# Expert and mark tables of a routed FFN's load loop interleaved, and six words of a step pair read by one load

## The chip, the cores and the metric

One core of one Trainium2 chip runs the whole program. The metric is the device time of one execution in microseconds (us). The runs of the kernel before took 1639.86, 1643.22 and 1646.82 us, median 1643.22.

## The reference

One layer on 512 latent tokens and 256 context tokens of width 1024: a bidirectional gated linear recurrence (HGRN2), then an expert FFN, then a final RMS norm. The part that matters here is the expert FFN: each token goes to 4 of 32 experts.

```python
logits = (h @ router_w + router_b)
top_v, top_i = lax.top_k(logits, 4)
top_w = softmax(top_v)
# for the tokens of an expert e:
z_glu, z_lin = split(h[tok] @ w1[e] + b1[e])        # w1[e]: 1024 x 2048
act = z_glu * sigmoid(1.702 * z_glu) * (z_lin + 1)   # both halves clamped at 7
y = act @ w2[e] + b2[e]                              # w2[e]: 1024 x 1024
```

The results are added per token with their weights. All is float32, so an expert's weights are 12 MB (8 MB of w1, 4 MB of w2) and those of all 32 are 384 MB.

## The kernel before

**Stages.** The recurrence and the router take the first 520 us or so. Then comes the expert loop, up to about 1592 us, and last the sum of the four results per token and the norm.

**Blocks, steps and two sides.** Tokens are grouped by expert in blocks of 32 slots (`G`). The 32 experts are put in two lists of 16 in an order worked out on the chip, by their number of blocks. One list goes through the *even* steps (`par` 0), whose weights lie in `arena`; the other through the *odd* steps (`par` 1), whose weights lie in `big_b`. A pair of steps is one turn of the loops `Fori(0, n_pairs)` that TensorE, VectorE, ScalarE, GpSimd (POOL) and SyncE (SP) each run; here it has 42 turns, 84 steps. An expert with several blocks stays in its side's buffer for several turns.

**The slots.** A side holds one expert in 12 slots of 1 MB: eight for w1 (`w1_slot`), four for w2 (`w2_slot`). In a step TensorE (L1805 to L1829) uses the last two w1 slots of the step (`z_chunk`, L1788), adds the bias (L1812), runs the first six w1 slots of the next step, which is the other side's, and then the four w2 slots of its own (L1826). After each slot it raises `w1_used` or `w2_used`, and before each it waits for that slot's load semaphore (`ld_w1`, `ld_w2`).

**SP's loop** (L475 to L505) issues the weight loads of both sides, one queue, in program order. At the head of each step it reads four words with `entry(1)` and `entry(2)` (L478 to L484): the expert of the next step and whether it is new there (the *mark*), and the same of the step after that, which is this side's next. They come from two tables of 192 words in one partition, `tab_l` (experts, clamped to 31) and `tab_new` (marks). A `value_load` with `min_val` and `max_val` is a load into a register followed by a check. After the head: `over_w1(0, 6)` waits for each of this side's first six w1 slots to be used and loads the side's next expert into it (L487 to L490, issued at L429), if the mark says that it is new; otherwise it only raises the load semaphore (L491 to L494). Then the same for the four w2 slots of the other side (L497 to L504, issued at L435), then `over_w1(6, 8)`.

**The tables** are written by VectorE before the loop (L1340 to L1348), from `bef`, the expert of each step: `tab_e`, `tab_l`, `tab_nf` and from it `tab_new`; `tab_ok` releases SP. SP gets there after its early weight loads (L444 to L471).

**POOL** gathers the token rows of the step after next (L621, into `xg`; VectorE transposes them at L1234 for TensorE) and scatters the results (L627).

Of the kernel before, what the change touches and what calls it, by code (L numbers as in the profile page):

```python
# [7 lines left out]
I32 = mybir.dt.int32  # L8
U32 = mybir.dt.uint32
F32R = mybir.dt.float32r  # L10
ALU = mybir.AluOpType
# [11 lines left out]
E, TOPK = 32, 4  # L23
# [4 lines left out]
NBT = 2 * NPAIR_MAX + 4  # L28
# [9 lines left out]
NW = D // QT  # L38
# [24 lines left out]
def build(nc, x, c, ctx_in, c_ctx, mod_c, mod_w, mod_b, norm1_g, norm2_g, hg_w_in, hg_lb_logits, hg_norm_g,  # L63
# [7 lines left out]
    with ExitStack() as stack:  # L71
        place = {}

        def sb(name, shape, dt=F32):
            place[name] = -(-nc.sbuf_base // 32) * 32
            return stack.enter_context(nc.sbuf_tensor(name, shape, dt))
# [20 lines left out]
        at = [0]  # L97
# [49 lines left out]
        res = sb("res", [P, 2, TOK], BF16)  # L147
# [26 lines left out]
        def rtake(n):  # L174
            at2[0] += n
            return ring_t[:, at2[0] - n:at2[0]]
# [21 lines left out]
        def half(n):  # L198
# [15 lines left out]
        bef = sb("bef", [P, NBT])  # L214
        ed_t = bef[0:E, 0:E]
        tab_e = sb("tab_e", [1, NBT], I32)
        tab_l, tab_new = (nc.alloc_sbuf_tensor_at(n, [1, NBT], I32, offset=place["res"] + 4 * NW + 4 * i * NBT)
                          for i, n in enumerate(("tab_l", "tab_new")))
        tab_nf = rtake(NBT)[0:1]
        tab_nn = sb("tab_nn", [1, 2])  # L220
        tab_n = sb("tab_n", [1, 2], I32)
# [117 lines left out]
        def _(sp):  # L339

            row = 0
            for v in (c[0], c_ctx, mod_b, norm1_g, hg_lb_logits[0, 0], hg_lb_logits[0, 1],
                      hg_lb_logits[1, 0], hg_lb_logits[1, 1], hg_norm_g):
                n = v.shape[0] // P
# [83 lines left out]
            def load_w1(par, e, pos):  # L428
                sp.dma_start(w1_slot(par, pos), moe_w1[bass.ds(e * D + pos * P, P), :]  # L429
                             ).then_inc(ld_w1[par][pos], 16)  # L430

            def load_w2(par, e, k):
                to = w2a[:, 2 * k:2 * k + 2, :] if par == 0 else \
                    big_b[:, B2_AT[k], :].rearrange("p (a n) -> p a n", a=2)
                sp.dma_start(to, moe_w2[bass.ds(e * FF + 2 * k * P, 2 * P), :].rearrange("(a p) n -> p a n", p=P)  # L435
                             ).then_inc(ld_w2[par][k], 16)
# [36 lines left out]
            n_pairs = sp.value_load(tab_n[0:1, 0:1], min_val=1, max_val=NPAIR_MAX)  # L473

            with sp.Fori(0, n_pairs) as i:  # L475
                for par in range(2):

                    def entry(n):  # L478
                        at = bass.ds(i * 2 + (par + n), 1)
                        return (sp.value_load(tab_l[0:1, at], min_val=0, max_val=E - 1),  # L480
                                sp.value_load(tab_new[0:1, at], min_val=0, max_val=1))

                    e_next, new_next = entry(1)
                    e_over, new_over = entry(2)  # L484

                    def over_w1(first, last):
                        with sp.If(new_over):  # L487
                            for pos in range(first, last):
                                sp.wait_ge(S["w1_used"], i * (2 * W1C) + (par * W1C + pos + 1))
                                load_w1(par, e_over, pos)  # L490
                        with sp.Else():  # L491
                            for pos in range(first, last):
                                sp.wait_ge(S["w1_used"], i * (2 * W1C) + (par * W1C + pos + 1))
                                sp.sem_inc(ld_w1[par][pos], 16)  # L494

                    over_w1(0, AHEAD)
                    with sp.If(new_next):  # L497
                        for k in range(W2C):
                            sp.wait_ge(S["w2_used"], i * (2 * W2C) + (par * W2C + k + 1))
                            load_w2(1 - par, e_next, k)  # L500
                    with sp.Else():
                        for k in range(W2C):
                            sp.wait_ge(S["w2_used"], i * (2 * W2C) + (par * W2C + k + 1))
                            sp.sem_inc(ld_w2[1 - par][k], 16)  # L504
                    over_w1(AHEAD, W1C)  # L505
# [373 lines left out]
        def _(dve):  # L879
            V = nc.vector  # L880
            me = Steps(dve, S["dve_s"])
# [409 lines left out]
            for i in range(LT):  # L1291
# [47 lines left out]
            dve.wait_ge(S["tab_ps"], 6)  # L1339
            me.link(V.tensor_scalar(bef[:, :], ps[7][:, 0:NBT], float(E), None, ALU.add))  # L1340
            me.mark(V.tensor_copy(tab_e[:, :], bef[0:1, :]))
            me.mark(V.tensor_scalar(tab_l[:, :], bef[0:1, :], float(E - 1), None, ALU.min))
            me.mark(V.tensor_tensor(tab_nf[:, 2:NBT], bef[0:1, 2:NBT], bef[0:1, 0:NBT - 2], ALU.not_equal))
            me.wait()
            me.link(V.scalar_tensor_tensor(tab_nf[:, 2:NBT], bef[0:1, 2:NBT], float(E) - 0.5, tab_nf[:, 2:NBT],
                                           ALU.is_lt, ALU.mult))
            me.link(V.tensor_copy(tab_new[:, :], tab_nf))
            dve.sem_inc(S["tab_ok"], 1)  # L1348
            dve.wait_ge(S["xi_ps"], 2)
            index(1, False)  # L1350
# [57 lines left out]
            me = Steps(dve, S["fin_s"])  # L1408
# [479 lines left out]
```

## Time and profile before

| | |
|---|---|
| median of the runs | 1643.22 us |
| profiled execution | 1641.11 us, span 1638.9 us |
| granted TensorE clock, mean | 0.951 of full |
| PE busy | 1485.2 us (91%) |
| DVE, ACT, POOL busy | 734.8 (45%), 251.8 (15%), 211.9 (13%) |
| bytes moved by DMA | 497.14 MB, mean 303 GB/s |
| weight loads, L429 and L435 | 384 issues of 1024 KB |
| chain that ended last | PE 62%, DMA 22%, SPq 9%, DVE 4%, issue 3% |

Engines: PE is TensorE, DVE VectorE, ACT ScalarE, POOL GpSimd; SPq is SyncE's instruction queue, which has no busy time of its own, since it only issues, waits and computes registers. The busy share is an average over stages with different limits; the chain of waits is followed back from the last instruction. Times in a timeline are microseconds from the start of the span. A transfer in the chain reaches from its issue to its landing, with what it waits for other transfers of its queue counted in. A matmul in float32 is two instructions in the trace, so a slot's four matmuls are eight rows.

### The profile page before, as it was taken

The numbers are of one execution on the slowest core, as the hardware profiler recorded it, in microseconds if no ns is written. First come the engines' busy times: TensorE is split into PE (matmuls) and PEld (weight loads), VectorE is DVE, ScalarE is ACT, GpSimd is POOL, SyncE is SP. The second block draws the span as 40 slices with busy tenths as digits, with TensorE's granted clock in tenths as the row PEclk, the third lists the DMA queues.
The fourth block names the chain that finished last, engine by engine and source line by source line (L and its number), as shares of the span: only waits on it lengthen the run. The fifth ranks groups of instructions, "written<-read, shape, count | busy, mean of one in ns | idle before, by whom it ended". The sixth has DMA issues, their size and how long they took to land.

```text
span 1638.9 us, 40839 instructions
## 1 busy us (share of the span) xinstructions
PE 1485.2 (91%) x14640; PEld 739.0 (45%) x14640; DVE 734.8 (45%) x2468; ACT 251.8 (15%) x434; POOL 211.9 (13%) x263
## 2 busy tenths in 40 slices
PE   5999999999894988999899799999788979898897
PEld 3658888888552332333244234333233323343233
DVE  4403877776747442434244244434233424343344
ACT  4403554554322000000000000000000000000001
POOL 1000000000250111212121111212111211111120
PEclk9999999999996998999799799999899989999898
DMA  8685111112767898948989989999899989999788
GB/s 358 194 269 146 52 52 51 51 51 55 277 266 265 338 419 320 417 199 337 414 325 400 414 336 400 417 414 412 320 418 416 417 324 410 417 413 417 298 323 310
DMA packets 130870, 497.14 MB, mean 303 GB/s; under 512 B 15372, under 2 KB 48492, under 8 KB 94908
## 3 DMA queue, kind: packets, MB, share of 16 engines
q1 hardware_dynamic: 122588, 479.99, 74.3%
q0 software_dynamic: 8256, 16.81, 2.8%
q8 instruction: 16, 0.26, 0.1%
q14 instruction: 10, 0.08, 0.0%
HBM read 484.92 MB, written 17.58 MB: 307 GB/s over the span
## 4 chain that ended last, share of the span: by engine, by line
PE 62%; DMA 22%; SPq 9%; DVE 4%; issue 3%; ACT 1%; POOL 0%; DVEq 0%; POOLq 0%; ACTq 0%
PE ps L1788 22%; PE ps L1826 12%; DMA arena<-in_moe_w 10%; DMA big_b<-in_moe_w 10%; PE ps L1485 6%; PE ps L1487 5%; PE ps L1486 5%; SPq L435 3%; SPq L429 3%; PE ps L1664 2%; PE ps L1596 1%; PE ps L1508 1%; DMA ring_t<-in_mod_c 1%; PE ps L1610 1%; PE ps L1605 1%
## 5 line engine op out<-in xcount | busy, mean ns | idle before, releaser
L1788 PE MATMUL ps<-arena,rows 128*32 128x512 f32 x2736 | 330.2, 617 | 41.8 <-DMA arena<-in_moe_w 33.4
L1788 PE MATMUL ps<-big_b,rows 128*32 128x512 f32 x2688 | 318.7, 609 | 29.6 <-DMA big_b<-in_moe_w 29.2
L1788 PEld LDWEIGHTS ps<-arena,rows 128*32 128x32 f32 x2736 | 86.4, 112 | 239.3 <-issue 151.2
L862 ACT ACTIVATE rows<-ps 128x256 f32<-128x256 f32 x84 | 32.3, 385 | 1050.1 <-issue 566.3
L1788 PEld LDWEIGHTS ps<-big_b,rows 128*32 128x32 f32 x2688 | 85.0, 111 | 220.2 <-issue 149.0
L1826 PE MATMUL ps<-big_b,rows 128*32 128x256 f32 x2688 | 166.4, 398 | 15.3 <-DMA big_b<-in_moe_w 15.3
L1826 PE MATMUL ps<-arena,rows 128*32 128x256 f32 x2688 | 167.0, 400 | 13.8 <-DMA arena<-in_moe_w 13.8
L1403 DVE SCALAR_TENSOR_TENSOR y_sb<-ps,w_s,g_q 128x256 f32<-128x256 f32 x42 | 20.3, 484 | 293.2 <-PE ps L1826 293.2
L1403 DVE SCALAR_TENSOR_TENSOR rows<-ps,w_s,g_q 128x256 f32<-128x256 f32 x42 | 20.3, 484 | 279.0 <-PE ps L1826 279.0
L1826 PEld LDWEIGHTS ps<-big_b,rows 128*32 128x32 f32 x2688 | 84.2, 114 | 77.6 <-DMA big_b<-in_moe_w 21.7
L1826 PEld LDWEIGHTS ps<-arena,rows 128*32 128x32 f32 x2688 | 84.8, 114 | 75.7 <-DMA arena<-in_moe_w 20.3
L621 POOL DMA_INDIRECT rows<-frows,tok_n x86 | 88.6, 1030 | 105.4 <-issue 59.2
L1485 PE MATMUL ps<-aT_hi,wh_hi 128*128 128x512 f32 x256 | 101.7, 397 | 0.0
L1487 PE MATMUL ps<-aT_hi,wh_lo 128*128 128x512 f32 x256 | 99.8, 390 | 0.0
L1486 PE MATMUL ps<-aT_lo,wh_hi 128*128 128x512 f32 x256 | 99.8, 390 | 0.0
L627 POOL DMA_INDIRECT yrows<-y_sb,row_s x43 | 44.2, 1029 | 421.0 <-issue 421.0
L627 POOL DMA_INDIRECT yrows<-rows,row_s x43 | 45.0, 1047 | 413.1 <-issue 412.2
L1273 DVE TENSOR_SCALAR pt<-slot_io,dm_all 128x128 bf16<-128x128 f32 x344 | 75.3, 282 | 33.2 <-issue 33.2
L563 POOL TENSOR_SCALAR xv_t<-xv_t 96x1024 f32<-96x1024 f32 x1 | 2.8, 2791 | 433.5 <-DMA xv_t<-in_moe_b 433.5
L1487 PEld LDWEIGHTS ps<-aT_hi,wh_lo 128*128 128x128 f32 x256 | 48.0, 188 | 10.3
L1485 PEld LDWEIGHTS ps<-aT_hi,wh_hi 128*128 128x128 f32 x256 | 48.1, 188 | 10.0
L1486 PEld LDWEIGHTS ps<-aT_lo,wh_hi 128*128 128x128 f32 x256 | 48.1, 188 | 9.1
(361 smaller groups left out, 1769.6 us busy)
## 6 DMA issues: line engine op xcount, KB each, us to landing
big_b<-in_moe_w SPq DMA_DIRECT2D x192, 1024.0 KB, 15.4
arena<-in_moe_w SPq DMA_DIRECT2D x192, 1024.0 KB, 16.7
ring_t<-in_hg_w_in SPq DMA_DIRECT2D x32, 512.0 KB, 3.9
ogT<-in_mod_w SPq DMA_DIRECT2D x16, 1024.0 KB, 5.1
arena<-yrows SPq DMA_DIRECT2D x8, 1024.0 KB, 12.0
x_sb<-in_x SPq DMA_DIRECT2D x2, 2048.0 KB, 7.9
arena<-in_hg_w_in SPq DMA_DIRECT2D x4, 1024.0 KB, 21.0
arena<-in_mod_c SPq DMA_DIRECT2D x4, 1024.0 KB, 22.3
```

Source lines behind the costliest of these rows:

```text
L429: sp.dma_start(w1_slot(par, pos), moe_w1[bass.ds(e * D + pos * P, P), :]).then_inc(ld_w1[par][pos], 16)
L435: sp.dma_start(to, moe_w2[bass.ds(e * FF + 2 * k * P, 2 * P), :].rearrange("(a p) n -> p a n", p=P)).then_inc(ld_w2[par][k], 16)
L621: pool.indirect_dma_start(out=xg[par], out_offset=None, in_=fquarters, in_offset=bass.IndirectOffsetOnAxis(ap=tok_n[par][:, :], axis=0), b ...
L627: pool.indirect_dma_start(out=yquarters, out_offset=bass.IndirectOffsetOnAxis(ap=row_s[par][:, :], axis=0), in_=y_sb[par], in_offset=None, ...
L1273: V.tensor_scalar(to[:, i, :], slot_io[:, :], dm_all[:, i, e], None, ALU.is_equal)
L1403: V.scalar_tensor_tensor(y_sb[par], ps[4 + par][:, 0:NW], w_s[par][:, :], g2_q[:, :], ALU.mult, ALU.mult).then_inc(S["y_ok"], 1)
L1485: mm(bank, th, mh, start=start, stop=False)
L1486: mm(bank, th, ml, start=False, stop=False)
L1487: return mm(bank, tl, mh, start=False, stop=stop)
L1664: last = mm(ps[YO_BANK[j]][:, :], ogT[:, k, i * P:(i + 1) * P], wo[n][:, k, :], start=(k == 0), stop=(k == DK - 1))
L1788: last = mm(bank[q * G:(q + 1) * G, :], XT[par][:, pos * G:(pos + 1) * G], w[:, :, q * NW:(q + 1) * NW], start=(pos == 0), stop=False)
L1826: last = mm(y[q * G:(q + 1) * G, 0:NW], aT2[:, (2 * m + a) * G:(2 * m + a + 1) * G], w2_slot(par, m, a)[:, q * NW:(q + 1) * NW], start=(m ...
```

## The change

- `tab_l` and `tab_new` become one table `tab_words`, two words per step (expert, mark), with two words of room in front, in the same place.
- VectorE writes the two halves with a step of two words; values are the same.
- SP no longer reads four words at the head of each step; it reads six words at the head of each pair, with one load instruction into six registers: expert and mark of steps 2i+1, 2i+2 and 2i+3. The even step uses words 0 to 3, the odd step 2 to 5.
- The check of each value against its bounds is left out.

```diff
--- before.py
+++ after.py
@@ -214,8 +214,8 @@
         bef = sb("bef", [P, NBT])
         ed_t = bef[0:E, 0:E]
         tab_e = sb("tab_e", [1, NBT], I32)
-        tab_l, tab_new = (nc.alloc_sbuf_tensor_at(n, [1, NBT], I32, offset=place["res"] + 4 * NW + 4 * i * NBT)
-                          for i, n in enumerate(("tab_l", "tab_new")))
+        tab_words = nc.alloc_sbuf_tensor_at("tab_words", [1, 2 * NBT + 2], I32, offset=place["res"] + 4 * NW)
+        tab_ld = tab_words[:, 2:2 * NBT + 2].rearrange("p (b w) -> p b w", w=2)
         tab_nf = rtake(NBT)[0:1]
         tab_nn = sb("tab_nn", [1, 2])
         tab_n = sb("tab_n", [1, 2], I32)
@@ -473,15 +473,13 @@
             n_pairs = sp.value_load(tab_n[0:1, 0:1], min_val=1, max_val=NPAIR_MAX)
 
             with sp.Fori(0, n_pairs) as i:
+                _, words = nc.values_load_multi_w_load_instructions(
+                    tab_words[0:1, bass.ds(i * 4 + 4, 6)], engines=[mybir.EngineType.SP], min_val=0, max_val=E - 1,
+                    skip_runtime_bounds_check_because="experts are clamped to E - 1 and marks are 0 or 1 where written")
                 for par in range(2):
 
-                    def entry(n):
-                        at = bass.ds(i * 2 + (par + n), 1)
-                        return (sp.value_load(tab_l[0:1, at], min_val=0, max_val=E - 1),
-                                sp.value_load(tab_new[0:1, at], min_val=0, max_val=1))
-
-                    e_next, new_next = entry(1)
-                    e_over, new_over = entry(2)
+                    e_next, new_next = words[2 * par:2 * par + 2]
+                    e_over, new_over = words[2 * par + 2:2 * par + 4]
 
                     def over_w1(first, last):
                         with sp.If(new_over):
@@ -1339,12 +1337,12 @@
             dve.wait_ge(S["tab_ps"], 6)
             me.link(V.tensor_scalar(bef[:, :], ps[7][:, 0:NBT], float(E), None, ALU.add))
             me.mark(V.tensor_copy(tab_e[:, :], bef[0:1, :]))
-            me.mark(V.tensor_scalar(tab_l[:, :], bef[0:1, :], float(E - 1), None, ALU.min))
+            me.mark(V.tensor_scalar(tab_ld[:, :, 0], bef[0:1, :], float(E - 1), None, ALU.min))
             me.mark(V.tensor_tensor(tab_nf[:, 2:NBT], bef[0:1, 2:NBT], bef[0:1, 0:NBT - 2], ALU.not_equal))
             me.wait()
             me.link(V.scalar_tensor_tensor(tab_nf[:, 2:NBT], bef[0:1, 2:NBT], float(E) - 0.5, tab_nf[:, 2:NBT],
                                            ALU.is_lt, ALU.mult))
-            me.link(V.tensor_copy(tab_new[:, :], tab_nf))
+            me.link(V.tensor_copy(tab_ld[:, :, 1], tab_nf))
             dve.sem_inc(S["tab_ok"], 1)
             dve.wait_ge(S["xi_ps"], 2)
             index(1, False)
```

## Rows read from the trace of the kernel before

**Rows 1.** TensorE's waits, 540 to 1592: waiter, releaser: us in total, times, longest.
```profile
PE ps L1788 <- DMA arena<-in_moe_w: 33.4, 28, 2.3
...
PE ps L1788 <- DMA big_b<-in_moe_w: 29.2, 26, 2.3
...
PE ps L1826 <- DMA big_b<-in_moe_w: 15.3, 16, 1.5
...
PE ps L1826 <- DMA arena<-in_moe_w: 13.8, 15, 1.5
```

**Rows 2.** Stretches: length, busy us by engine, clock, DMA share, GB/s.
```profile
547.00:645.00 98.00, 82.98 (x932) 28.91 (x924) 32.45 (x149) 2.70 (x7) 14.37 (x14) 0.91 0.98 400
...
953.00:1080.00 127.00, 122.23 (x1496) 48.06 (x1492) 51.60 (x236) 4.22 (x11) 22.59 (x22) 0.97 1.00 407
...
1185.00:1344.00 159.00, 136.46 (x1564) 48.79 (x1556) 52.22 (x239) 4.23 (x11) 22.58 (x22) 0.92 1.00 409
...
1352.00:1445.00 93.00, 88.82 (x1080) 33.99 (x1076) 36.88 (x167) 3.08 (x8) 16.44 (x16) 0.96 1.01 412
...
1553.00:1592.00 39.00, 39.00 (x504) 16.01 (x500) 15.38 (x71) 1.15 (x3) 6.17 (x7) 1.00 0.82 333
...
716.00:745.00 29.00, 29.00 (x368) 11.46 (x364) 13.71 (x62) 1.15 (x3) 6.16 (x6) 1.00 0.06 20
```

**Rows 3.** Timeline 843 to 849: start, us, engine, line, operation, count.
```profile
845.50 4.05 PE L1788 MATMUL ps<-big_b,rows 128*32 128x512 f32 x36
...
848.39 0.35 SPq L429 DMA_DIRECT2D big_b<-in_moe_w  x1
```

**Rows 4.** Timeline 1180 to 1187, TensorE and SP.
```profile
1181.20 5.33 PE L1788 MATMUL ps<-arena,rows 128*32 128x512 f32 x48
...
1184.77 2.23 SPq L429 DMA_DIRECT2D arena<-in_moe_w  x4
```

**Rows 5.** Chain of waits, 900 to 1010: start, us, queue, line.
```profile
919.75 0.07 SPq L475
...
922.35 0.05 SPq L487
...
923.45 0.05 SPq L499
...
923.71 0.39 SPq L435
```

**Rows 6.** Lines 480 and 481 on SP: count: ns min/median/max, first and last.
```profile
L480 SPq TENSOR_LOAD <-tab_l x168: 262/270/589, 538.8 to 1582.8; - x168
...
L481 SPq FUSED_REGOPS  x168: 147/147/157, 539.8 to 1584.0; - x168
```

**Rows 7.** Timeline 505 to 548, VectorE, the second table write.
```profile
520.02 0.25 DVE L1347 CAST tab_new<-ring_t 1x192 int32<-1x192 f32 x1
```

**Rows 8.** Timeline of SP's transfers, 530 to 1600; x is how many were issued.
```profile
536.33 0.37 SPq L435 DMA_DIRECT2D arena<-in_moe_w  x1
...
536.74 0.99 SPq L435 DMA_DIRECT2D big_b<-in_moe_w  x2
...
546.63 5.63 SPq L429 DMA_DIRECT2D big_b<-in_moe_w  x8
...
1017.76 8.38 SPq L429 DMA_DIRECT2D big_b<-in_moe_w  x8
...
1445.53 8.00 SPq L429 DMA_DIRECT2D arena<-in_moe_w  x8
```

**Rows 9.** Line 429, loads of w1: time from issue to landing.
```profile
DMA to landing us min/median/max: 4.7/15.1/26.0
```

**Rows 10.** Timeline 814 to 824, a gather and the transpose that uses it.
```profile
814.29 1.04 POOL L621 DMA_INDIRECT rows<-frows,tok_n  x1 [0.70 <-issue]
...
822.48 0.43 DVE L1234 STREAM_TRANSPOSE rows<-rows 128x256 f32<-128x256 f32 x1
```

**Rows 11.** Line 621, the gathers: time from issue to landing.
```profile
DMA to landing us min/median/max: 2.6/6.0/6.7
```

## The prediction

> **What bounds the kernel now.** I read four views, in this order. The waits of TensorE in the expert loop name one releaser only, the weights: 33.4 + 29.2 + 15.3 + 13.8 = 91.7 us in 85 waits [rows 1]. So the loop is either at TensorE's own pace or waiting for weights. Cutting the loop by hand into stretches shows that these alternate [rows 2]. In a stretch with weights the 16 DMA engines are full (share 0.98 to 1.01, 400 to 412 GB/s) and TensorE is idle for part of it: 15.0 us of 547 to 645, 4.8 of 953 to 1080, 22.5 of 1185 to 1344, 4.2 of 1352 to 1445. Between them lie dry stretches, 716 to 745 the longest, with 20 GB/s and TensorE never idle: the experts in work need no new weights, and both buffers are full. The reader is to see that nothing can be gained inside a full stretch (the bytes set it) and nothing inside a dry one (TensorE sets it), but that the end of a dry stretch counts: when the first load of the next expert is issued earlier, the whole train of loads behind it lands earlier, and the wait that ends the train shrinks by as much. I call such a point a restart.
>
> What holds a restart back is seen in the timeline. At 845.50 TensorE starts the 48 matmuls of six chunks that use up six slots; the first 36 take 4.05 us, so a chunk of eight takes 0.90 us and the first slot is free at 846.40. The first load into it is issued by SP at 848.39 [rows 3]. At the next restart of the other buffer it is 1181.20 + 0.89 (48 in 5.33 us, six chunks) = 1182.09 against 1184.77 [rows 4]. SP is late by 2.0 and 2.7 us. What it does in that time is the head of the step, read off the chain of waits where it shows a whole one: from the top of the loop at 919.75 to the first branch at 922.35, 2.60 us [rows 5].
>
> **What the change removes.** A head has four table loads. Each is a load of 0.27 us (median of 168, two such groups), a register operation of 0.147 us [rows 6], and an assertion, an address and gaps for the rest of 0.62 us; four make 2.5, and with the loop's own 0.1 the 2.60 above. Over 84 steps that is 84 x 2.5 = 210 us of SP's time; it is not the gain, since SP mostly waits or is blocked.
>
> **What it adds.** One load of six words per pair of steps. No row shows a load of more than one word. Lower bound: as one word, 0.27. Upper bound: six single ones, 1.6, the words being fetched one after the other. The longest single one was 0.59 [rows 6]. I take 0.4, near the single row, since what an instruction of this kind spends is mostly its trip; without the checks one register wait of up to 0.15 may stay. So the head of an even step (arena, behind the loop's branch) goes from 2.6 to some 0.5, and that of an odd step (big_b) to nothing.
> A rule of the Trainium skill speaks against this: "Runtime: NRT & Kernel Launch", section Instruction fetch mechanics, puts a register load at about 200 ns per register even in bulk, though from HBM; by it the six words would be an estimated 1.2 us and the sum below 2.4 us smaller. No row here shows which holds. Another, in "DMA: Bandwidth & Descriptors", Latency and other measured facts, puts the floor of such a load at some 600 ns; the trace does not agree, 0.262.
>
> The two table writes on VectorE get a step of two words. The second takes 0.25 us [rows 7]; if the stride costs up to as much again, that is 0.5 us for both, and less than nothing is excluded, as no element falls away. They are done at 520.3, while SP is busy with earlier weights until 537.73 [rows 8] and reads the tables only then: I take nothing. If SP came sooner, they would cost 0.5 us once.
>
> **What a restart gains.** The release of a slot to the issue costs SP a computed address, a move and the issue: 923.45 to 923.71 where the chain shows it, 0.3 us with the semaphore [rows 5].
> - Odd step: possible at 846.40 + 0.3 = 846.7, was 848.39: **1.7 us**.
> - Even step: the slot allows 1182.4. SP's head began at 1184.77 - 0.4 - 2.6 = 1181.8; with 0.5 and 0.4 it issues at 1182.7: **2.1 us**.
>
> Which first loads are restarts follows from counting. An expert is 12 loads of 1.049 MB, 2.57 us each at 408 GB/s; the quickest load landed 4.7 us after its issue [rows 9]. A train of n loads begun at T is thus through at T + 4.7 + 2.57(n - 1), and the next load lands 2.57 later or 4.7 after its own issue, whichever is later. Only in the second case does the issue matter. SP's timeline has 16 first issues that qualify or come close; going through them:
> - 546.63 (odd). Three loads from 536.33 on end near 546.2; the next could land at 548.7, but 546.63 + 4.7 = 551.3 [rows 8]. Two heads lie between SP's last early issue and this one, 2.1 + 2.5 = 4.6 us earlier: limited by the queue to 2.6, I take **2.4**.
> - 650.80 and 744.41 (odd, dry before): **1.7** each.
> - 848.39 (odd), then 881.76 (even): 848.39 + 33.0 = 881.4, the queue just runs out, so the even restart decides: **2.1**.
> - 952.46, 985.67, 1017.76: each 33 us on, the queue just empty each time. At 1017.76 (odd, [rows 8]) pace alone gives 1021.2, the issue 1022.5; the lead passes through and the odd one caps it: **1.7**.
> - 1080.83, then 1112.77 (odd): the same, **1.7**.
> - 1184.77 (even, dry): **2.1**. Its train runs on to 1344; at 1243.40 and 1277.27 the queue is not empty, nothing more.
> - 1351.23 (even, dry): **2.1**.
> - 1445.53 (even, [rows 8]): 36 loads from 1351.23 end at 1445.9, the next by pace 1448.5, by issue 1450.2; part of the three trains was blocked by a full queue, so I take **1.0**.
> - 1552.41 (even, dry): TensorE is busy in 39.0 of the last 39.0 us [rows 2], nobody waits for this train: **0**.
>
> Sum: 2.4 + 1.7 + 1.7 + 2.1 + 1.7 + 1.7 + 2.1 + 2.1 + 1.0 = **16.5 us**. Each is smaller than TensorE's idle time in its train (4.2 us at least), so none is lost to the pace of TensorE. The gains add, because after each train TensorE sets the time of the next restart from the landing before it. The profiled execution took 1641.1 us (span 1638.9 and 2.2 around it): 1624.6. The median of the runs, 1643.2, is 2.1 above it; less 16.5 it is **1626.7, I say 1627**.
>
> **Rivals.**
> 1. The words are fetched one by one, 1.6 us. The even head is then 0.1 + 1.6 + 0.15 instead of 2.6, the even restart gains 0.9 and not 2.1. The three even ones that decide lose 3 x 1.2 = 3.6, the odd ones nothing: gain 13, 1630. For it: no row of a multi-word load; against: 0.27 for one word cannot tell trip from words. Chance 0.17.
> 2. The transfers don't move. The first load may be late for a reason that a shorter head leaves: a stall of SP at the branch into the rarely run issuing arm, or a train paced by slots and not by the queue. For it: the chain of waits never names the head at a restart. Against: that chain follows a late load to its own issue and counts the queue before it as transfer, so it can't name it. Gain 0 to 8 us, 1635 to 1643. Chance 0.15.
> 3. Slower: the gathers. POOL fetches the next rows right at a restart (814.29, used at 822.48, 8.2 us [rows 10]); in dry stretches such a gather has the engines for itself, and now 1.7 to 2.1 us more of each restart's weights stand before it. From a landing of over 8.2 us on, TensorE waits in every step in a full stretch. Landings are 2.6 to 6.7 us at present, those of full stretches included [rows 11], so it would take 1.5 us more than the worst. If each of some 45 steps in full stretches lost 0.7 us, that is 31 less 16: 1658. Chance 0.03.
> 4. The removed checks are put back by the build, so that only the loads merge. Then six register operations with their assertions stay, 6 x 0.2 = 1.2 us on the even head, and the odd restarts gain all the same: like the first rival, 1629. It shares its chance.
>
> **How the numbers follow.** Forecast 0.65, within 1622 to 1632. The first rival (and fourth) adds 1629 to 1633, the second 1635 to 1643, the third above. About half of the second must be left out: 1619 to 1638. Under 0.5% (8.2 us, about what a measurement tells from no change) falls most of rival 2 and a thin end of the others: faster 0.80, same 0.16, slower 0.04.
>
> **What would show it.** The last stretch (1553 to 1592) has TensorE never idle as before, and the dry stretches keep their length less 1.7 to 2.1 us each. First issues come 1.2 us after the start of the six chunks at odd restarts and 1.5 at even ones, in place of 2.9 and 3.6. TensorE's 91.7 us of waits fall to about 75; matmul times, bytes and the full rate stay. A table load group of 42, once per pair, shows its length: 0.4 or 1.6 decides rival 1. I am wrong if the first issues move and the waits don't, or if waits for the gathers' transpose appear.

## The result, and the profile after

The changed kernel takes 1628.0 us (median, 1624.45 to 1632.99), the kernel before 1642.5 (1639.86 to 1646.82) beside it: a ratio of 0.9926, 95% interval 0.9903 to 0.9950. That is 12.2 us less by the ratio, 8.2 to 15.9 by its interval; the medians alone differ by 14.5. 1627 was predicted, from a sum of 16.5. So the gain came out at three quarters of the sum, and that the median lies within 1 us of 1627 is in part luck.

The profiled execution took 1632.99 us with a span of 1630.8. The first rows of its page, busy time and the 40 slices, differ from those of the kernel before in a place here and there only:

```profile
PE 1487.4 (91%) x14640; PEld 742.2 (46%) x14640; DVE 737.1 (45%) x2468; ACT 251.7 (15%) x434; POOL 211.8 (13%) x263
...
PE   5999999999995997999799799999889979998897
...
PEclk9999999999997997999899799999798989998898
...
DMA  8685111112767798957989989999899989999778
...
GB/s 359 201 266 146 52 52 51 51 51 56 267 258 287 317 419 334 417 215 325 414 338 404 414 340 402 417 415 418 332 417 416 417 329 417 417 413 417 314 309 307
```

TensorE's waits in the expert loop, as in [rows 1]:

```profile
PE ps L1786 <- DMA arena<-in_moe_w: 33.4, 27, 2.3
...
PE ps L1786 <- DMA big_b<-in_moe_w: 24.9, 22, 2.2
...
PE ps L1824 <- DMA arena<-in_moe_w: 11.7, 14, 1.5
...
PE ps L1824 <- DMA big_b<-in_moe_w: 11.5, 14, 1.5
```

They add up to 81.5 us, 10.2 less than 91.7; a fall to about 75 was predicted. The reader is to see that busy times say nothing here (PE 1487.4 against 1485.2, at a mean granted clock of 0.945 against 0.951); the time went out of the waits for weights.

The first issues in SP's timeline, as in [rows 8]:

```profile
544.18 6.05 SPq L429 DMA_DIRECT2D big_b<-in_moe_w  x8
...
947.23 10.10 SPq L429 DMA_DIRECT2D big_b<-in_moe_w  x8
...
1012.42 10.11 SPq L429 DMA_DIRECT2D big_b<-in_moe_w  x8
...
1072.38 9.74 SPq L429 DMA_DIRECT2D arena<-in_moe_w  x8
...
1435.54 9.76 SPq L429 DMA_DIRECT2D arena<-in_moe_w  x8
```

And an odd and an even restart, each with the bias matmul, which starts 0.22 us before the six chunks, as in [rows 3, 4]. First the odd one, then the even one:

```profile
842.61 0.40 PE L1810 MATMUL ps<-bias,sel 96*32 96x512 bf16 x4
...
844.10 1.19 SPq L429 DMA_DIRECT2D big_b<-in_moe_w  x2
```

```profile
1175.97 0.40 PE L1810 MATMUL ps<-bias,sel 96*32 96x512 bf16 x4
...
1177.82 0.96 SPq L429 DMA_DIRECT2D arena<-in_moe_w  x2
```

The first load now follows the start of the bias matmul by 1.49 us at an odd step and by 1.85 at an even one. In the kernel before it was 3.11 and 3.79, read in the same way (bias at 845.28 and 1180.98). So odd restarts come 1.62 us earlier relative to TensorE and even ones 1.94; 1.7 and 2.1 had been worked out. The load of six words:

```profile
L476 SPq TENSOR_LOAD <-tab_words x42: 714/720/1088, 540.5 to 1563.0; - x42
```

It took 0.72 us (the median; the three numbers are least, median and most in ns), between the 0.4 taken and the 1.6 of the first rival.

### The profile page after: what moved, and what is told of

Read it like the earlier page. It is cut to its first block, busy times and chain, and to the rows that moved or that the text cites. A ratio compares the mean times of both kernels' runs of the same rounds, so it can differ in the third digit from the quotient of the medians.

```text
span 1630.8 us, 39663 instructions
## 1 busy us (share of the span) xinstructions
PE 1487.4 (91%) x14640; PEld 742.2 (46%) x14640; DVE 737.1 (45%) x2468; ACT 251.7 (15%) x434; POOL 211.8 (13%) x263
## 4 chain that ended last, share of the span: by engine, by line
PE 65%; DMA 20%; SPq 8%; DVE 4%; issue 2%; ACT 1%; POOL 0%; DVEq 0%; POOLq 0%; ACTq 0%
PE ps L1786 25%; PE ps L1824 12%; DMA big_b<-in_moe_w 9%; DMA arena<-in_moe_w 8%; PE ps L1483 6%; PE ps L1484 5%; PE ps L1485 5%; SPq L435 5%; SPq L429 2%; PE ps L1662 2%; PE ps L1506 1%; PE ps L1594 1%; DMA ring_t<-in_mod_c 1%; PE ps L1603 1%; PE ps L1608 1%
## 5 line engine op out<-in xcount | busy, mean ns | idle before, releaser
L1824 PEld LDWEIGHTS ps<-big_b,rows 128*32 128x32 f32 x2688 | 84.8, 114 | 74.0 <-DMA big_b<-in_moe_w 17.2
L1485 PEld LDWEIGHTS ps<-aT_hi,wh_lo 128*128 128x128 f32 x256 | 48.1, 188 | 10.2
```

Of the source, the lines that this page charges most:

```text
L1485: return mm(bank, tl, mh, start=False, stop=stop)
L1824: last = mm(y[q * G:(q + 1) * G, 0:NW], aT2[:, (2 * m + a) * G:(2 * m + a + 1) * G], w2_slot(par, m, a)[:, q * NW:(q + 1) * NW], start=(m ...
```

## The experiments

Where trains are compared, the start of a step's bias matmul marks the step, and I take the time from one such start to another, against the same in the kernel before. The 84 steps are counted from 0. All kernels are edits of the changed one, except `four_unchecked`, which is one of the kernel before. Ratios are to the kernel before, run beside each of them. The loop has to be read apart from the rest: step 0 starts between 533.4 and 541.3 us in the 14 profiles, and three of them (`one_checked`, `pause_middle`, `pause_even16`) have a wait of 7.3 to 8.7 us for the first transposed rows at 530 us, before the loop.

**Once more.** `after_again` is the changed kernel.

> The changed kernel once more, for how far one execution's trains of loads differ from another's. Theory (the gain is made at the restarts, where the first load into a freed slot is issued 1.6 us earlier at odd steps and 1.9 us at even ones): 12 to 16 us faster than before, first issues 1.3 us (odd) and 1.6 us (even) after the start of the six chunks as in the first profile. Two trains (from 648 and the end of the one from 947) gave back 0.9 and 1.6 us there by chance, through TensorE's granted clock and single landings; if that is chance, other trains do it here. Rival (the small gain of those trains is systematic): the same two give back again.

Measured: ratio 0.9931 (0.9916 to 0.9946), 1629.9 us, which is 11.3 us faster, a little under the 12 to 16 expected. The trains, with the four repeats told of below, are in the table of the next section. Of the two suspected trains, that from 947 to 1171 lacked its second gain again and in every repeat, so this is systematic; the gain of the one from 648 varied from 0.2 to 2.7 us, so there it is chance.

**Only the checks go.**

```diff
-                        return (sp.value_load(tab_l[0:1, at], min_val=0, max_val=E - 1),
-                                sp.value_load(tab_new[0:1, at], min_val=0, max_val=1))
+                        return tuple(nc.values_load(t[0:1, at], engines=[SP], min_val=0, max_val=top,
+                                                    skip_runtime_bounds_check_because=...)
+                                     for t, top in ((tab_l, E - 1), (tab_new, 1)))
```

> Only the checks go: four loads of one word at the head of each step, as before, two separate tables, none checked. A head should shrink from 2.6 to about 1.4 us. Theory: every restart gains 1.15 us, odd or even, nine of them, times the 0.85 that the whole change gave of its sum: some 9 us faster than before, 1633. Rival A (the loads are the cost, the checks wait beside them): under 3 us faster. Rival B (all of SP's instructions count, 218 us of them were removed for 14 us): 84 x 1.15 = 97 us of SP's time less, so 6 us faster.

Measured: 0.9964 (0.9949 to 0.9979), some 6 us faster (3.4 to 8.4 by the interval); the loop of its one profile is 8.5 us shorter. The even restart:

```profile
1174.32 0.40 PE L1813 MATMUL ps<-bias,sel 96*32 96x512 bf16 x4
...
1177.19 0.69 SPq L429 DMA_DIRECT2D arena<-in_moe_w  x2
```

is 2.87 us after the bias, not 3.79; odd ones 2.2, not 3.1. So the four checks cost 0.9 us of a head, not 1.15, and about half of the whole change's gain comes from them. Rival A falls. Rival B is not refuted here: its 6 us are what the runs gave, the theory's 9 lie outside the interval. With the 0.9 us of a head put in for 1.15 the theory says 7. What decides between them is the pair `checked_head` and `checked_middle`.

**Only the merging.**

```diff
                 _, words = nc.values_load_multi_w_load_instructions(
-                    tab_words[0:1, bass.ds(i * 4 + 4, 6)], engines=[SP], min_val=0, max_val=E - 1,
-                    skip_runtime_bounds_check_because=...)
+                    tab_words[0:1, bass.ds(i * 4 + 4, 6)], engines=[SP], min_val=0, max_val=E - 1)
```

> Only the merging: one load of six words per pair, but all six words checked. The even head should be 0.1 + 0.75 + 6 x 0.2 = 2.05 us, the odd head nothing. Theory: odd restarts gain 1.6 us as in the whole change (the first, two alone, one each in two trains: 2.5 + 4 x 1.6), even ones 0.5 (three), about 11 us by the sum and 9 to 10 measured: 1633. Rival B (SP's time in all): 210 - 42 x 2 = 126 us less of SP's time, 8 us faster. The two differ in where: by the theory the odd first issues come 1.3 us after the start of the six chunks and the even ones 3.0.

Measured: 0.9951 (0.9937 to 0.9964), 8.0 us, which is again rival B's number (8) and less than the theory's 9 to 10; the loop of its one profile is 6.1 us shorter. Where the gain lies is as the theory has it: the odd ones are at 1.49, and the even restart comes late:

```profile
1181.59 0.40 PE L1809 MATMUL ps<-bias,sel 96*32 96x512 bf16 x4
...
1185.08 0.97 SPq L429 DMA_DIRECT2D arena<-in_moe_w  x2
```

That is 3.49 us after the bias (3.2 was expected): six checks cost an even head 1.6 us, so the merging with checks gives an even step only 0.3 us.

**Only the interleaving.** Four checked loads of one word from the interleaved table.

```diff
-                e_next, new_next = words[2 * par:2 * par + 2]
+                def entry(n):
+                    return tuple(sp.value_load(tab_words[0:1, bass.ds(i * 4 + (2 * (par + n) + 2 + w), 1)],
+                                               min_val=0, max_val=top) for w, top in ((0, E - 1), (1, 1)))
```

> Only the interleaving: the tables are written with a step of two words, SP reads four single words per step with checks as before. Theory: nothing moves against before, within 0.3%; the two writes on VectorE end long before SP reads them. Rival (the layout matters, through the writes or through where the words lie): any clear difference, up to the whole gain.

Measured: 0.9996 (0.9985 to 1.0008). The layout and the two strided writes change nothing, within 2.5 us, as forecast.

**Four pauses that were none.** `pause_head`, `pause_middle`, `pause_odd16` and `pause_even16` were to put unchecked loads back at chosen places:

```diff
+                    for _ in range(8):
+                        nc.values_load(tab_words[0:1, 2:3], engines=[SP], ..., skip_runtime_bounds_check_because="a pause")
```

> The changed kernel with eight single-word loads more at the head of each step, behind the read of the words: some 2.4 us per head, 84 x 2.4 = 200 us of SP's time, about what the change had removed. Theory (only the lateness at a restart counts): odd first issues come 1.7 us later, even ones 2.4, and the time of the kernel before comes back, 1641 to 1645. A rival that puts the gain down to the checks or to the number of single-purpose instructions would see nothing of it come back.

> The same eight loads in each step, but behind over_w1(0, 6), where SP is waiting for TensorE to use the w2 slots or is blocked by the full queue. Theory: SP has this time to spare and the transfers of the train are already queued, so nothing comes back: within 1.5 us of the changed kernel, 1628 to 1631. Rival (SP's instruction time in all is what counts, wherever it lies): the same as pause_head, 1641 or more.

> Sixteen such loads at the head of odd steps alone, 4.8 us; odd first issues come 4.1 us later than in the changed kernel. Theory, by trains (a train being the loads from one dry stretch to the next), against the changed kernel: the loads from 544 on lose 3, those from 648 and 741 4.1 each, the one from 844 1 to 2 (an even restart follows in it), the one from 947 4.1 and again 3 at its later odd restart, that from 1178 3 at its odd restart, that from 1343 none at first and 2 to 3 later: 24 to 27 us, 1653 to 1656. Rival (every head counts alike): 42 x 4.8 = 200 us.

> The same at the head of even steps alone; even first issues come 4.8 us later. Theory: the trains from 648 and 741, whose restarts are odd and which have no even one that is not covered by a full queue, lose nothing; those from 1178 and 1343 lose 4.8 each, the one from 844 some 4 at its even restart, the others 3 to 4 each: 25 to 30 us, 1654 to 1659. The pattern by trains is the opposite of pause_odd16. If a train with no restart of that side loses time, the theory is wrong.

Measured: 0.9946, 0.9932, 0.9937 and 0.9940. None of the expected losses came, and the traces say why: the only table load in their loops is the one of six words, 42 times, and each has 39663 instructions, as many as the changed program. The loads whose values nothing used were dropped when the program was built. They test no theory; they are four more executions of the changed program, and are used as such.

**The pauses, with checks.** A checked load stays. `checked_head` has four in each head, `checked_middle` the same four behind `over_w1(0, AHEAD)`:

```diff
+                    for _ in range(4):
+                        sp.value_load(tab_words[0:1, bass.ds(i * 4 + 4, 1)], min_val=0, max_val=E - 1)
```

> The loads of the four pauses before this were dropped when the program was built, as nothing used their values; those four kernels ran the changed program. Here the pause is four single-word loads with checks, 2.5 us, at the head of each step, beside the read of six words: the four loads of the kernel before, come back. Theory (lateness at the restarts is all that counts): first issues 3.1 us (odd) and 4.3 (even) after the bias of the step, where the kernel before has 3.1 and 3.8; the time is that of the kernel before or 1 to 2 us above it, 1640 to 1643. Rival (the gain comes from the layout or the one load itself): stays at 1629.

> The same four checked loads, 2.5 us in each of the 84 steps, but behind over_w1(0, 6), where SP waits for the w2 slots or is blocked by the full queue. Theory: first issues stay at 1.5 and 1.9 us after the bias, nothing comes back, within 1.5 us of the changed kernel: 1628 to 1631. Rival (SP's instruction time in all counts, 210 us of it): as checked_head, 1640 or more.

Measured: `checked_head` 1.0013 (0.9998 to 1.0029), the kernel before again; `checked_middle` 0.9925 (0.9901 to 0.9949), nothing back. Head, then middle, at the same restart, and the loads of the pause in the middle:

```profile
1181.87 0.40 PE L1812 MATMUL ps<-bias,sel 96*32 96x512 bf16 x4
...
1186.05 0.96 SPq L429 DMA_DIRECT2D arena<-in_moe_w  x2
```

```profile
1173.69 0.40 PE L1812 MATMUL ps<-bias,sel 96*32 96x512 bf16 x4
...
1175.54 0.35 SPq L429 DMA_DIRECT2D arena<-in_moe_w  x1
```

```profile
L496 SPq TENSOR_LOAD <-tab_words x336: 263/268/331, 541.4 to 1577.1; - x168
```

Both have the same 336 loads and nearly the same time of SP's: from one load to the next 0.57 us at the head and 0.56 in the middle (medians), so some 190 us, not 210. At the head they make the first issue 4.18 us late, in the middle it stays at 1.85. The medians differ by 14.6 us. This pair decides against rival B: it is not how long SP works that counts but where in the step. That only those heads count at which the queue is dry is the matter of the next run.

**Late at odd steps only.** Eight checked loads at the head, `if par == 1`; 5.0 us were reckoned, the trace has 0.55 us from one to the next, 4.4 in all.

> Eight such loads, 5.0 us, at the head of odd steps alone: odd first issues 5.6 us after the bias and not 1.5, 4.1 later; even ones stay at 1.9. Theory, by trains against the changed kernel: loads from 544 on lose 3, from 648 4, from 741 4, from 844 1 (an even restart follows), from 947 to 1171 7 (two odd restarts with dry queues before them), from 1178 3 (an odd restart late in it), from 1343 to its first wait 0, later 3: 25 us, 1653 to 1656. Rival (every head counts alike): 42 x 5.0 = 210 us. If the even-led stretch from 1343 to 1384 loses time, the theory is wrong.

Measured: 1.0042 (1.0022 to 1.0062); the loop is 17.2 us longer than the mean of the six executions of the changed program, not 25. Odd first issues are 5.24 us after the bias, 3.75 later than in the changed kernel and not 4.1:

```profile
850.97 0.40 PE L1813 MATMUL ps<-bias,sel 96*32 96x512 bf16 x4
...
856.21 0.98 SPq L429 DMA_DIRECT2D big_b<-in_moe_w  x2
```

By trains, against that mean: 2.9 (3 expected), 5.0 (4), 3.1 (4), 2.0 (1), 4.0 (7), 0.2 (3), -1.3 (0), 1.3 (3). 42 pauses of 4.4 us cost 17 us and not 185, so heads do not count alike, and the even-led train loses nothing. Two terms came out 1 us too large, which is what single trains vary by. But the three that came out small are all of one kind: a later restart within a train, where by my counting the queue has just run empty.

**A step further.** `words_ahead` has no load in any head:

```diff
+            ahead = [[sp.alloc_register(f"ahead{p}_{w}") for w in range(4)] for p in range(2)]
+            sp.reg_load(ahead[0], tab_words[0:1, 4:8])
             with sp.Fori(0, n_pairs) as i:
...
+                    words = [sp.snap(r, min_val=0, max_val=E - 1) for r in ahead[par]]
...
                     over_w1(0, AHEAD)
+                    sp.reg_load(ahead[1 - par], tab_words[0:1, bass.ds(i * 4 + (6 + 2 * par), 4)])
```

> A step further: eight lasting registers; each step's four words are read one step ahead, by one unchecked load of four words behind over_w1(0, 6) of the step before, so that no head has a load at all. The load (some 0.55 us) lies where SP waits. Theory: odd first issues stay at 1.5 us after the bias, even ones come at 1.5 in place of 1.9; 0.35 us at four or five even restarts, 1 to 1.5 us faster than the changed kernel, which a timing here can hardly tell; the trace shows it in the first issues. Rival: anything beyond 3 us either way.

Measured: 0.9923 (0.9902 to 0.9943), 1626.8 us. The even restart is at 1.49, the odd's value, and the load of four words is of 0.59:

```profile
1169.66 0.40 PE L1810 MATMUL ps<-bias,sel 96*32 96x512 bf16 x4
...
1171.15 1.19 SPq L429 DMA_DIRECT2D arena<-in_moe_w  x2
```

```profile
L494 SPq TENSOR_LOAD <-tab_words x84: 294/594/901, 537.3 to 1570.0; - x84
```

It is the lowest ratio of all, but `checked_middle`, beside it on the same chip, had 1626.7: it beats the kernel before, not demonstrably the changed one.

## Why the prediction was right, and where it was not

The changed program was profiled six times. The stretches between the waits that end the trains, from bias matmul to bias matmul, against the one profile of the kernel before, in us:

| steps | restarts (before) | predicted | mean of six | least and most |
|---|---|---|---|---|
| 0 to 8 | 546.63 | -2.4 | -2.5 | -2.5, -2.6 |
| 8 to 13 | 650.80 | -1.7 | -1.5 | -0.2, -2.7 |
| 13 to 20 | 744.41 | -1.7 | -1.5 | -0.7, -2.0 |
| 20 to 32 | 848.39, 881.76 | -2.1 | -1.0 | -0.3, -1.5 |
| 32 to 51 | 952.46 to 1112.77 | -3.4 | -1.3 | -0.6, -1.6 |
| 51 to 63 | 1184.77 | -2.1 | -1.4 | -0.9, -1.6 |
| 63 to 68 | 1351.23 | -2.1 | -2.2 | -1.0, -3.4 |
| 68 to 83 | 1445.53, 1552.41 | -1.0 | -0.6 | +0.5, -1.7 |
| sum | | -16.5 | -12.0 | -9.8, -13.0 |

The kernel before has only one profile. `interleaved_four_checked`, whose SP does the same work in the same time, gives a second: in order of the rows it differs from the first by +0.1, +0.5, -0.4, +0.8, +0.4, +0.6, -0.9 and -0.2. So a single row is good to some 0.8 us. Against the mean of these two profiles, 20 to 32 gains 1.4, 32 to 51 1.5, 51 to 63 1.7 and 63 to 68 1.7, and the sum is 12.4: of the shortfalls only that of 32 to 51 is well above the noise.

The prediction's time came out closer than its sum. 16.5 was the sum, 12.0 to 12.4 the loops show, 12.2 the ratio; the five later timings of the same program gave 8.9 to 11.3 us.

**The mechanism stands.** The gain is made at restarts (`checked_head` against `checked_middle`), in the trains named, by the lateness worked out from the rows, and none that 2.5 us would show comes from the layout (`interleaved_four_checked`).

**The price of the six-word load** was 0.72, not 0.4: an even restart gained 1.94 and not 2.1. Rival 1 (the words one by one) is nearer to the truth in kind than in size: from one word (0.27) to six (0.72) each further word costs 0.09 us. Sum effect: under 1 us. The Trainium skill's rule of about 200 ns per register ("Runtime: NRT & Kernel Launch", Instruction fetch mechanics), stated for loads from HBM, gave an estimated 1.2; this load, from on-chip memory, does not follow it, with its 0.72 for six registers.

**The step that failed is the count that calls a queue "just empty".** I took the 16 engines as one queue emptied at a mean pace of 2.57 us per load and let 1017.76, 1080.83, 1112.77 and 1445.53 be restarts. The trace of before could have told. The stretch of 3 us at each such first issue, columns as in [rows 2] (the last two are the DMA share and GB/s):

```profile
881.00:884.00 3.00, 3.00 (x36) 0.98 (x32) 0.96 (x5) 0.00 (x0) 0.00 (x0) 1.00 0.62 167
...
985.00:988.00 3.00, 3.00 (x36) 0.98 (x32) 0.96 (x5) 0.00 (x0) 0.00 (x0) 1.00 0.75 242
...
1017.00:1020.00 3.00, 3.00 (x32) 0.70 (x24) 1.43 (x8) 0.00 (x0) 0.19 (x1) 1.00 1.01 371
...
1080.00:1083.00 3.00, 3.00 (x36) 0.83 (x32) 0.96 (x5) 0.00 (x0) 0.00 (x0) 1.00 1.02 393
...
1112.00:1115.00 3.00, 3.00 (x32) 0.79 (x24) 1.58 (x8) 0.00 (x0) 0.34 (x1) 1.00 1.00 337
...
1445.00:1448.00 3.00, 3.00 (x36) 0.97 (x32) 0.96 (x5) 0.00 (x0) 0.00 (x0) 1.00 1.04 400
```

The DMA share is 0.62 and 0.75 at 881 and 985, but 1.01, 1.02, 1.00 and 1.04 at the four others: the engines were still at work. The landing records of the same trace say it in times, in us after the issue:

| first issue | the load before it lands | it lands itself |
|---|---|---|
| 881.76 | 0.6 | 4.8 |
| 985.67 | 1.3 | 4.8 |
| 1017.76 | 2.2 | 5.0 |
| 1080.83 | 2.5 | 5.4 |
| 1112.77 | 2.5 | 5.3 |
| 1445.53 | 3.7 | 6.2 |

The last four land 2.4 to 2.9 us after the load before them, at the pace of a running queue: not the time of the issue but the landing before it set those (1017.76 is a tie of both, which an earlier issue can't shorten either). What was mis-sized is the pace. Between the first and the last landing of a train it is 2.63 to 2.68 us per load, not 2.57; over the 36 loads from 1351.23 that makes 3.3 us, and the last lands at 1449.27 where the prediction had 1445.9. The 2.57 came from 408 GB/s, the rate of all transfers, in which the token rows of the gathers and scatters are counted; that these make up the difference is argued, not tested.

After the change the same is seen: the train from 952.46 starts 5.23 us earlier (947.23), its first issue of 1080.83 comes 8.45 us earlier (1072.38), yet TensorE reaches step 51 only 5.01 us earlier (1175.97 for 1180.98). The first loads of 952.46, 1080.83 and 1112.77 land 5.0, 5.1 and 5.0 us earlier than before: the lead won at the first restart is kept, and the extra 3.2 us of the issue bought nothing. The term was -3.4 for two gains where there was one, 1.3 (1.5 against the mean of two profiles), and -1.0 at 1445.53 for -0.6, with a spread as large as itself. `checked_odd8` shows it from the other side: 4.0 for 7, 0.2 for 3, 1.3 for 3.

At 881.76 the engines were in part dry before, and less so after (share 0.93), probably since the train before it had also been brought forward; 1072 is as full as its forerunner:

```profile
876.00:879.00 3.00, 3.00 (x36) 0.93 (x28) 2.45 (x9) 0.04 (x1) 1.15 (x2) 1.00 0.93 273
...
1072.00:1075.00 3.00, 3.00 (x32) 0.84 (x28) 2.22 (x9) 0.00 (x0) 1.03 (x1) 1.00 1.03 410
```

The gain there was 1.0 of 2.1 (1.4 against the mean of the two profiles). By the landing records of the two first profiles the first engine delivered that restart's load 4.79 us earlier than before and the last one 3.97, against 2.67 by which TensorE was ahead; so 2.1 and 1.3. Why the 16 engines lay 1.2 us apart there and 0.3 before stays open.

**What made single trains vary.** The end of the train from 650.80, before and after:

```profile
697.78 1.07 PE L1788 MATMUL ps<-big_b,rows 128*32 128x512 f32 x8 [1.67 <-DMA big_b<-in_moe_w]
...
700.63 1.06 PE L1788 MATMUL ps<-big_b,rows 128*32 128x512 f32 x8 [1.79 <-DMA big_b<-in_moe_w]
```

```profile
696.19 1.07 PE L1786 MATMUL ps<-big_b,rows 128*32 128x512 f32 x8 [1.91 <-DMA big_b<-in_moe_w]
...
698.87 1.94 PE L1786 MATMUL ps<-big_b,rows 128*32 128x512 f32 x8 [1.61 <-DMA big_b<-in_moe_w]
```

The last eight matmuls of the wait took 1.06 us before and 1.94 after. The granted clock there was 1.00 (700.6 to 701.7) before and 0.50 (698.8 to 700.7) after, the lower of the two levels, 1.2 GHz; TensorE had stood idle for a load just before in both, 1.79 and 1.61 us. From 540 to 1590 the kernel before had the lower level in 17 pieces of the trace, 123 us in all, the changed one in 16, 130 us. The slower matmuls are 0.9 of the 1.5 us missing in this train's first profile; in the repeats it fell otherwise. Only mean values over several profiles say something about one train.

**The slots themselves** may cost the odd restarts a little. In the kernel before, SP came late and found slots free, so it issued the first loads every 0.6 us; now it issues them as TensorE frees the slots, 0.9 us apart (SP's rows "x8" last 10.1 us, not 8.5). The train from 648.29 delivered its second load only 2.1 us ahead of the kernel before, where the first issue was 2.5 ahead. Argued from one train's landing records, not tested.

Rival 2 (transfers don't move) and rival 3 fell: the longest gather landed after 7.3 us in place of 6.7, still under the 8.2 at which it would be late, and no wait for its transpose appeared in the loop but one of 0.4 us at its start, which the kernel before has too. Rival 4 (checks put back) is seen not to be so: no assertion stands at line 476 in the changed kernel, while `one_checked` has 252 there.

## What to carry to other kernels

In a loop whose queue alternates between full and dry, price a delay of the issuing engine only where the queue runs dry: count such points, multiply by the lateness at each, and ignore the rest of that engine's time, however long. To tell whether a point is dry, read the DMA share of the two or three microseconds at the issue itself, or when the load before it lands, rather than counting transfers at a mean pace: an error of 3% in the pace is 3 us after 36 loads. When a time fits two theories, as `four_unchecked` and `one_checked` did, move the same work to another place. And before believing a pause that costs nothing, look in the trace whether it is there.

## What the runs showed of the hardware

A register load from on-chip memory on SP took 0.27 us for one word, 0.59 for four and 0.72 for six, medians of 168, 84 and 42: about 0.1 us per further word. The check of a word cost 0.23 us (four checks 0.9, by the lateness of `four_unchecked` against the kernel before) to 0.27 (six, 1.6, `one_checked`). Against an even head without any load (`words_ahead`, 1.49 us), the one load of six words delays the first issue by 0.4 us (1.85), four plain loads of one word by 1.4 (2.87). A checked load of one word followed the one before it after 0.55 to 0.57 us (`checked_odd8`, `checked_middle`, `checked_head`).
